# State space layer: the sample states' products in one run over four row groups of the array, and part of the next group's convolution work moved between the squares

## The chip, the cores and the metric

One core of a Trainium2 chip runs the whole program. The metric is device time in microseconds (us), the median of several runs. TensorE multiplies matrices, VectorE and ScalarE do element-wise work, GpSimd does element-wise work and starts some transfers, and SyncE (SP) starts the loads and stores from its queue, in order.

## The reference, cut to what matters

A decoder step of two layers for a prompt (512 tokens) and for 8 samples of 8 new tokens each, which share all weights; all in 32 bit floats. The change is in the state space mixer of the first layer. Per group (8 groups of 4 heads of 64 columns, 128 states):

```python
xc = silu(conv_b + sum(xpad[:, k:k + l] * conv_w[k] for k in range(4)))   # x (two blocks of 128), B, C
xw = (exp(a_cum[:, -1:] - a_cum) * dt)[..., None] * x
states = einsum('bcsgn,bcsgjp->bcgjpn', B, xw)
h = chunk_decay[..., None, None] * h + states        # per sample: the new state, 8 samples of 8 tokens
y = (wts @ x) + (C @ h_prev) * exp(a_cum) + d_skip * x
gz = y * silu(z); gz = gz * rsqrt(mean(gz * gz) + eps) * norm_g
out = gz @ w_out
```

For the samples the state of each of the 8 samples gets the sum over its own 8 tokens of B times the weighted x. The 64 sample tokens lie beside the 512 prompt tokens, 576 columns in all.

## The kernel before, in words

Every engine has its own program; semaphores join them. In the state space stage, `group(g)` is run for 8 groups: 0 by itself, 1 to 6 as a hardware loop ("the middle groups"), 7 by itself. While a group's own work is done, TensorE also projects the next group: six units of weights, `ahead(0)` to `ahead(5)`, 48 products of 288 columns each. It also projects the former group's output back (`back(0)`, `back(1)`, two units). The units' weights come from SP into two raw buffers. ScalarE rounds them (`high_part`, L939, called `proj(k)` for the units of `ahead(k)`). GpSimd takes the rest (`low_part`, L782), and TensorE needs both.

TensorE's order in a middle group is: `decays` (L1764), `back(0)` (L1966 to L1968), `sample_decays` (L1768), `ahead(0)`, `turn` (L1778, L1782), `ahead(1)`, `chunk_sums` (L1790, L1792, L1798), `back(1)`, `ahead(2)`, `outputs` (L1810 to L1833), `ahead(3)`, `states(g, 0)` (L1885), the first half of `ahead(4)`, `group_sums` (L1893), the rest of `ahead(4)`, `states(g, 1)`, `ahead(5)`. In `ahead`, L1523 and L1524 are the products with the rounded weights and L1531 those with the rest.

The 64 sample tokens take rows 0 to 63. A tile `bd` (64 rows, 4 blocks of 128) holds B of each token in one of four blocks and zero in the other three. `states` multiplies it with the weighted x in two row groups of 32 rows (4 samples each). So 8 samples take two calls of four products (each is two records in the trace, since these are 32 bit products), and each call writes banks 6 and 7 of PSUM. VectorE adds them to the states `h0` in between (`sample_states`, L2873). `decays` of the next group waits for the last of these additions, for the root (`gsqrt_ready`) and for `acm`.

At the end of a group: VectorE makes both halves of y (L2855 to L2864), which release ScalarE's squares (L1335); then VectorE takes `ahead(3)` out of PSUM (L2685 to L2687) and adds the squares (L2879, `gsum_done`). TensorE sums over them (L1893), ScalarE takes the root (L1343), VectorE the reciprocal (L2902). Then VectorE scales y, does `sample_states(1)`, `ahead(4)`, the low parts of the result `gl` (L2913), the convolution `conv(g + 1, 2)` and `ahead(5)`. ScalarE's order there: squares, `proj(5)`, root, `conv_out(g + 1, 0)` and `(g + 1, 1)` (L1254, L1258), `tap` 2 and 3 (L1270), `high_part` of the unit for the next `back(0)`, `gh` (L1355), `gate_out`, `conv_out(g + 1, 2)`.

One thread matters across engines. GpSimd's `new_conv_state` (L841) comes behind the low part of `proj(5)`. SP's queue has, in this order: the last unit of the group, the store of that convolution state (L659, waits for L841), the unit for the next `back(0)` (L565), the stores of the states. So that unit can't be asked for before L841 is done.

At the layer's start GpSimd clears the small tiles (L822, L823) once the constants are in, then copies the convolution state, then makes the first low part (L782). VectorE goes through `raw_dt`, the logarithm's series, the sums, `state_coefs`, `token_major` and `head_rows(0)` (L2714, gives `acm`), which the first `decays` waits for.

## Time and profile before

| | |
|---|---|
| time, 3 runs | 2462.85 us median (2460.12 to 2463.0) |
| span of the profiled execution | 2457.2 us |
| median less this span | 5.65 us |
| TensorE busy | 2421.8 us (99% of the span) |
| VectorE, ScalarE, GpSimd busy | 1856.6, 1391.8, 731.7 us |
| mean granted TensorE clock | 0.994 |
| period of a middle group | 66.4 us |

The profile is of one execution. Its span is from the first to the last instruction; of the profiled execution itself no time is given beside its span, so the 5.65 us are what the timed runs have around such a span. PE is TensorE's multiplying, PEld its loading of weights; POOL is GpSimd, DVE VectorE, ACT ScalarE.

### The profile page before, as it was taken

Reading aid. Unit: us, or ns where it says so; the run is one execution under the profiler, and the core shown is the slowest. Engines: PE = TensorE matmul, PEld = TensorE weight load, DVE = VectorE, ACT = ScalarE, POOL = GpSimd, SP = SyncE. Lnnn points to the kernel's source line nnn. Section 1 sums busy time; section 2 is a strip of 40 time slices with the busy share of each in tenths; the row PEclk is TensorE's granted clock in tenths of the full one; section 3 lists DMA queues with packets and bytes.
Section 4 is the critical chain, followed back from the end, with each engine's and each line's share of the span. In section 5 each row is a group of like instructions: output and inputs, shape, how many; then the busy total and the mean of one; then the engine's idle time right before and its main releaser. Section 6 shows DMA issues by size and latency. Waiting matters only on the chain.

```text
span 2457.2 us, 50185 instructions
## 1 busy us (share of the span) xinstructions
PE 2421.8 (99%) x19713; PEld 2363.8 (96%) x19713; DVE 1856.6 (76%) x3053; ACT 1391.8 (57%) x2388; POOL 731.7 (30%) x672
## 2 busy tenths in 40 slices
PE   8999999999999999999999999999999999999998
PEld 8999999889999989999999999999999997999998
DVE  8979767988888888978876988875235438988875
ACT  7757553645555556757665767664222227767663
POOL 1222233444454532222223222224322321222222
PEclk9999999999999998999999999999999999999999
DMA  6677743123333325677665676763443334677762
GB/s 191 163 169 172 167 119 114 47 95 106 105 101 102 97 88 132 167 160 172 159 146 128 161 168 165 173 150 124 157 141 124 136 110 105 161 170 163 173 149 89
DMA packets 105558, 339.00 MB, mean 138 GB/s; under 512 B 13648, under 2 KB 17232, under 8 KB 87056
## 3 DMA queue, kind: packets, MB, share of 16 engines
q1 hardware_dynamic: 53808, 242.38, 30.0%
q0 software_dynamic: 51552, 93.87, 22.7%
q8 instruction: 137, 2.24, 0.4%
q14 instruction: 61, 0.50, 0.1%
HBM read 223.04 MB, written 19.32 MB: 99 GB/s over the span
## 4 chain that ended last, share of the span: by engine, by line
PE 92%; DVE 4%; DMA 1%; ACT 1%; issue 0%; SPq 0%; DVEq 0%; ACTq 0%
PE ps L1627 17%; PE ps L1625 17%; PE ps L1635 17%; PE ps L1523 7%; PE ps L1531 7%; PE ps L1524 7%; PE ps L1644 2%; PE ps L1645 2%; PE ps L1652 2%; PE ps L1966 1%; PE ps L1967 1%; PE ps L1968 1%; PE ps L1574 1%; DMA sb_lw<-sb_rawf 1%; PE ps L1564 1%; PE ps L1565 1%
## 5 line engine op out<-in xcount | busy, mean ns | idle before, releaser
L1627 PE MATMUL ps<-sb_ual,sb_hw 128*128 128x288 f32 x2240 | 612.8, 295 | 0.0
L1625 PE MATMUL ps<-sb_uah,sb_hw 128*128 128x288 f32 x2240 | 609.5, 295 | 0.2
L799 POOL DMA_DIRECT2D sb_lw<-sb_rawf x328 | 282.2, 866 | 961.6 <-ACT sb_lw L970 944.9
L1625 PEld LDWEIGHTS ps<-sb_uah,sb_hw 128*128 128x128 f32 x2240 | 420.9, 188 | 0.9 <-issue 0.7
L1627 PEld LDWEIGHTS ps<-sb_ual,sb_hw 128*128 128x128 f32 x2240 | 421.2, 188 | 0.0
L1635 PE MATMUL ps<-sb_uah,sb_lw 128*128 128x288 f32 x2240 | 384.8, 293 | 1.1 <-DMA sb_lw<-sb_rawf 1.0
L782 POOL TENSOR_TENSOR sb_wl<-sb_raw,sb_wh 128x1024 fp32r<-128x1024 f32 (+1 forms) x106 | 259.2, 2449 | 412.6 <-ACT sb_wh L939 399.0
L1523 PE MATMUL ps<-sb_uh,sb_wh 128*128 128x288 f32 x1360 | 374.2, 302 | 0.4 <-DVE sb_zs L2707 0.2
L1524 PE MATMUL ps<-sb_ul,sb_wh 128*128 128x288 f32 x1360 | 366.6, 296 | 0.0
L1635 PEld LDWEIGHTS ps<-sb_uah,sb_lw 128*128 128x128 f32 x2240 | 327.9, 188 | 2.3 <-DMA sb_lw<-sb_rawf 1.8
L1523 PEld LDWEIGHTS ps<-sb_uh,sb_wh 128*128 128x128 f32 x1360 | 255.7, 188 | 10.3 <-issue 7.0
L968 ACT CAST sb_hw<-sb_rawf 128x512 fp32r<-128x512 f32 x336 | 207.7, 618 | 86.8 <-PE ps L1635 74.9
L1524 PEld LDWEIGHTS ps<-sb_ul,sb_wh 128*128 128x128 f32 x1360 | 255.8, 188 | 0.5
L1627 PE MATMUL ps<-sb_hl,sb_hw 128*128 128x288 f32 x896 | 244.0, 295 | 0.0
L1625 PE MATMUL ps<-sb_hh,sb_hw 128*128 128x288 f32 x896 | 243.2, 294 | 0.0
L939 ACT CAST sb_wh<-sb_raw 128x1024 fp32r<-128x1024 f32 (+1 forms) x106 | 111.9, 1056 | 176.5 <-PE ps L1531 120.8
L2328 DVE TENSOR_TENSOR sb_lw<-sb_tw,sb_hw 128x1024 fp32r<-128x1024 f32 x112 | 137.1, 1224 | 93.3 <-ACT sb_hw L1005 89.1
L970 ACT ACTIVATE sb_lw<-sb_rawf 128x512 fp32r<-128x512 f32 x328 | 206.4, 629 | 0.0
L1531 PE MATMUL ps<-sb_uh,sb_wl 128*128 128x288 f32 x1360 | 195.4, 296 | 0.0
L1005 ACT CAST sb_hw<-sb_tw 128x1024 fp32r<-128x1024 f32 x112 | 117.8, 1052 | 124.1 <-PE ps L1635 124.1
L1531 PEld LDWEIGHTS ps<-sb_uh,sb_wl 128*128 128x128 f32 x1360 | 186.1, 189 | 0.7 <-issue 0.7
L1627 PEld LDWEIGHTS ps<-sb_hl,sb_hw 128*128 128x128 f32 x896 | 168.4, 188 | 0.0
(357 smaller groups left out, 5118.2 us busy)
## 6 DMA issues: line engine op xcount, KB each, us to landing
sb_lw<-sb_rawf POOLq DMA_DIRECT2D x358, 256.0 KB, 3.7
sb_rawf<-w_ffn_in SPq DMA_DIRECT2D x87, 1024.0 KB, 5.0
sb_rawf<-w_ffn_so SPq DMA_DIRECT2D x32, 1024.0 KB, 5.0
sb_raw<-w_ssd SPq DMA_DIRECT2D x64, 512.0 KB, 3.6
sb_raw<-w_att SPq DMA_DIRECT2D x40, 512.0 KB, 3.7
sb_rawf<-w_ffn_out SPq DMA_DIRECT2D x32, 384.0 KB, 3.1
sb_h<-state SPq DMA_DIRECT2D x8, 1024.0 KB, 4.9
ssm_sample<-sb_h SPq DMA_DIRECT2D x8, 1024.0 KB, 4.8
```

The costliest lines, as they stand in the source:

```text
L782: pool.tensor_tensor(wl[parity][:, 0:width], raw[:, parity, 0:width], wh[parity][:, 0:width].bitcast(F32), ALU.subtract).then_inc(wl_done, 1)
L799: pool.dma_start(slot(lw, p), rawf[:, s % 2, i * BL:(i + 1) * BL], accum_op=ALU.add).then_inc(ld_in[i], 16)
L968: nc.scalar.copy(slot(hw, p), src).then_inc(hd_done, 1)
L970: nc.scalar.activation(slot(lw, p), src, ACT.Copy, scale=-1.0).then_inc(nd_done, 1)
L1005: nc.scalar.copy(slot(hw, 7, 2), tw[:, 2 * BL:4 * BL]).then_inc(ht34_done, 1)
L1523: pe.matmul(ps[:, b, 0:n], w, rh[:, k, t0:t0 + n], start=first and k == 0, stop=False)
L1524: pe.matmul(ps[:, b, 0:n], w, rl[:, k, t0:t0 + n], start=False, stop=False)
L1531: ins = pe.matmul(ps[:, b, 0:n], w, rh[:, k, t0:t0 + n], start=False, stop=last and k == nk - 1)
L1625: pe.matmul(out, w[:, k * P:(k + 1) * P], high[k], start=begins and k == 0, stop=False, skip_group_check=True)
L1627: pe.matmul(out, w[:, k * P:(k + 1) * P], low[k], start=False, stop=False, skip_group_check=True)
L1635: ins = pe.matmul(out, v[:, k * P:(k + 1) * P], high[k], start=False, stop=k == 3, skip_group_check=True)
L2328: V.tensor_tensor(slot(lw, 7, 2), tw[:, 2 * BL:4 * BL], slot(hw, 7, 2).bitcast(F32), ALU.subtract).then_inc(lt34_done, 1)
```

## The change

The sample tokens are spread over 128 rows: each sample takes 16 rows, of which 8 hold tokens and 8 are zero. Tiles `xsp` (x) and `bsp` (B) hold them in that form, and ScalarE writes them there in `conv_out`. A row group of 32 rows now holds two samples, `bd` needs two blocks instead of four, and one run of 8 products over four row groups gives all 8 samples' sums, into banks 4 to 7. The run stands behind `ahead(4)`, and waits for the root too, since banks 4 and 5 hold its sums. The other products and VectorE's instructions on sample tokens take 128 rows instead of 64.

In middle groups ScalarE does `conv_out(g + 1, 0)` between the two squares, `conv_out(g + 1, 1)` and `tap` 2 behind them, then the root, and `proj(5)` only behind the root. VectorE adds the squares before it takes `ahead(3)` out, then does `conv(g + 1, 2)`, and then the reciprocal; all four additions to the states come together behind the scaling.

At the layer's start GpSimd clears `xsp` (256 columns), part of `bt` (32 rows, 384 columns) and `bsp` (128 columns). VectorE makes three small copies in `state_coefs` into `bt`, and no longer clears `tok`.

```diff
+            bd = at("bd", [P, 2, NST])
+            xsp = at("xsp", [P, 2, P])
+        def spaced(ap):
+            return ap.rearrange("p (b s) -> p b s", s=2 * NS)[:, :, 0:NS]
+        def samples_of(i):
+            return bsp[:, :] if i == 2 else xsp[:, i, :]
-        def state_bank(half, rg, last):
-            return ((2, 3), (6, 7))[half][rg] if last else 6 + rg
+        def state_bank(rg, last):
+            return (2, 3, 6, 7)[rg] if last else 4 + rg
...
 GpSimd, ssd():
                 pool.memset(cz[:, :], 0.0)
+                pool.memset(xsp[:, :, :].rearrange("p i r -> p (i r)"), 0.0)
+                pool.memset(bt[0:HEADS, 0:3 * P], 0.0)
+                pool.memset(bsp[:, :], 0.0).then_inc(rows_zero, 1)
...
 ScalarE, conv_out and group:
-                    nc.scalar.activation(smp(xc[:, k, SEQ:TOK]), new, ACT.Silu, bias=bias).then_inc(xc_ready, 1)
+                    dst = smp(xc[:, k, SEQ:TOK]) if k == 3 else spaced(samples_of(k))
+                    nc.scalar.activation(dst, new, ACT.Silu, bias=bias).then_inc(xc_ready, 1)
+                    inside = not first and not last
                     for i in range(2):
                         act.wait_ge(gz_ready, g * 2 + (i + 1))
                         nc.scalar.activation(zs[:, i, :], ysb[:, i, :], ACT.Square).then_inc(gsq_done, 1)
-                    if not last:
+                        if inside:
+                            conv_out(g + 1, i)
+                    if inside:
+                        tap(g + 1, 2)
+                    elif first:
                         proj(5)
...
-                    if not last:
+                    if first:
                         conv_out(g + 1, 0)
                         conv_out(g + 1, 1)
                         tap(g + 1, 2)
+                    elif inside:
+                        proj(5)
+                    if not last:
                         tap(g + 1, 3)
...
 TensorE:
-                            ins = pe.transpose(ps[0:SMP, 4, rows(i)], xc[:, i, SEQ:TOK], ident[:, :])
+                            ins = pe.transpose(ps[:, 4, rows(i)], samples_of(i), ident[:, :])
-                    pe.matmul(ps[0:SMP, 4, 0:SMP], xc[:, 2, SEQ:TOK], xc[:, 3, SEQ:TOK],
+                    pe.matmul(ps[:, 4, 0:SMP], samples_of(2), xc[:, 3, SEQ:TOK],
-                def states(g, half, last=False):
+                def states(g, last=False, row_groups=(0, 1, 2, 3)):
...
-                    elif half == 0:
+                    else:
                         pe.wait_ge(y_evac, g * 2 + 2)
-                    else:
-                        pe.wait_ge(ss_evac, g * 4 + 2)
+                        pe.wait_ge(gsqrt_ready, g + 1)
                     for k in range(2):
-                        for rg in range(2):
+                        for rg in row_groups:
...
                     ahead(3)
-                    states(g, 0)
                     ahead(4, lambda: group_sums(g))
-                    states(g, 1)
+                    states(g)
                     ahead(5)
...
 VectorE:
-                    V.memset(tok[:, :, :, :].rearrange("p q c h -> p (q c h)"), 0.0)
-                    V.tensor_tensor(t2, t2, t0, ALU.mult).then_inc(dtok_in, 1)
+                    step(V.tensor_tensor(t2, t2, t0, ALU.mult))
+                    dve.wait_ge(rows_zero, 1)
+                    for q, src in enumerate((acT, t0, t2)):
+                        ins = V.tensor_copy(spaced(bt[0:HEADS, rows(q)]), smp(src[0:HEADS, SEQ:TOK]))
+                    ins.then_inc(dtok_in, 1)
...
-                    if not last:
+                    if first:
                         ahead(3)
...
                         V.tensor_tensor(zs[:, 0, :], zs[:, 0, :], zs[:, 1, :], ALU.add).then_inc(gsum_done, 1)
-                        sample_states(0)
                         if first:
                             conv(1, 1)
                             head_rows(1)
+                        else:
+                            ahead(3)
+                            conv(g + 1, 2)
...
-                        sample_states(1)
+                        sample_states(range(4))
                         ahead(4)
...
-                        conv(g + 1, 2)
+                        if first:
+                            conv(1, 2)
                         ahead(5)
```

## Rows read from the trace of the kernel before

**Rows 1.** The page's part 1: busy time of each engine and share of the span

```profile
PE 2421.8 (99%) x19713; PEld 2363.8 (96%) x19713; DVE 1856.6 (76%) x3053; ACT 1391.8 (57%) x2388; POOL 731.7 (30%) x672
```

**Rows 2.** Waits of TensorE, whole span: us in total, times, longest us

```profile
PE ps L1764 <- DVE sb_acm L2714: 3.6, 1, 3.6
...
PE ps L1764 <- DVE sb_h L2873: 1.1, 1, 1.1
```

**Rows 3.** Window table around groups 0 and 1; PEclk is the granted clock

```profile
434.00:488.00 54.00, 50.21 (x402) 45.97 (x400) 50.36 (x99) 32.92 (x61) 26.79 (x26) 0.97 0.15 43
```

**Rows 4.** The states' products, L1885: all records (ns min/median/max)

```profile
L1885 PEld LDWEIGHTS ps<-sb_xws,sb_bd x128: 181/184/185, 478.5 to 931.6; 32*128 32x128 f32 x128
```

**Rows 5.** TensorE in order of time around a run of `states` (group 1): start, us

```profile
549.59 0.56 PE L1531 MATMUL ps<-sb_uh,sb_wl 128*128 128x288 f32 x3
550.09 1.13 PE L1885 MATMUL ps<-sb_xws,sb_bd 32*128 32x256 f32 x8
...
551.38 0.29 PE L1524 MATMUL ps<-sb_ul,sb_wh 128*128 128x288 f32 x1
```

**Rows 6.** The chain that ended last, pieces in order of time: start, us

```profile
589.03 0.89 PE ps L1790 x8
589.92 0.26 PE ps L1792 x2
```

**Rows 7.** TensorE's weight loads in order of time, group 1 and its end

```profile
553.26 0.82 PEld L1893 LDWEIGHTS ps<-sb_zs,sb_ones 128*128 128x128 f32 x4
...
567.49 0.19 PEld L1966 LDWEIGHTS ps<-sb_gh,sb_wh 128*128 128x128 f32 x1 [0.36 <-issue]
...
574.02 0.18 PEld L1768 LDWEIGHTS ps<-sb_acm,sb_onr 64*128 64x128 f32 x1 [0.17 <-issue]
```

**Rows 8.** VectorE in order of time, end of group 1

```profile
551.00 1.53 DVE L2879 TENSOR_TENSOR sb_zs<-sb_zs 128x576 f32<-128x576 f32 x1
...
555.36 3.75 DVE L2902 RECIPROCAL sb_gnr<-sb_gnr 128x576 f32<-128x576 f32 x1 [1.63 <-ACT sb_gnr L1343]
...
560.70 1.28 DVE L2873 TENSOR_TENSOR sb_h<-sb_h,ps 128x512 f32<-128x512 f32 x2
```

**Rows 9.** ScalarE in order of time, end of group 1 and start of group 2

```profile
549.70 0.69 ACT L1335 ACTIVATE sb_zs<-sb_ysb 128x576 f32<-128x576 f32 x1 [2.15 <-DVE sb_ysb L2864]
...
554.58 0.74 ACT L1343 ACTIVATE sb_gnr<-ps,sb_eps 128x576 f32<-128x576 f32 x1 [1.96 <-PE ps L1893]
...
557.51 0.71 ACT L1254 ACTIVATE sb_xc<-sb_acc,sb_cw 128x512 f32<-128x512 f32 x1
...
560.33 1.05 ACT L939 CAST sb_wh<-sb_raw 128x1024 fp32r<-128x1024 f32 x1 [0.51 <-DMA sb_raw<-w_ssd]
...
572.33 1.14 ACT L1284 ACTIVATE sb_sg<-ps,sb_gtok 128x128 f32<-128x128 f32 x4
```

**Rows 10.** GpSimd in order of time, end of group 1

```profile
554.71 0.66 POOL L841 COPY sb_ncv<-sb_xp 128x27 f32<-128x27 f32 x4
561.47 2.42 POOL L782 TENSOR_TENSOR sb_wl<-sb_raw,sb_wh 128x1024 fp32r<-128x1024 f32 x1 [6.10 <-ACT sb_wh L939]
```

**Rows 11.** SP's queue in order of time, end of group 1

```profile
555.53 0.35 SPq L659 DMA_DIRECT2D conv_new<-sb_ncv  x1
556.47 0.34 SPq L565 DMA_DIRECT2D sb_raw<-w_ssd  x1
```

**Rows 12.** GpSimd, TensorE and VectorE at the layer's start

```profile
396.94 0.31 POOL L823 MEMSET sb_cz<- 128x256 f32 x1
...
397.79 4.76 POOL L782 TENSOR_TENSOR sb_wl<-sb_raw,sb_wh 128x1024 fp32r<-128x1024 f32 x2
...
400.33 0.31 PE L1531 MATMUL ps<-sb_uh,sb_wl 128*128 128x288 f32 x1
...
402.72 0.46 DVE L2685 TENSOR_TENSOR sb_xp<-ps,sb_rms 128x288 f32<-128x288 f32 x1 [1.92 <-PE ps L1531]
...
441.17 0.24 DVE L2676 COPY sb_tok<-ps 64x96 f32<-64x96 f32 x1
```

More of the change, by code:

```diff
@@ L266, in step_kernel @@
             mask = at("mask", [P, P])
-            masks = at("masks", [SMP, SMP])
-            maskb = at("maskb", [SMP, NB // 2])
+            masks = at("masks", [P, SMP])
+            maskb = at("maskb", [P, 2])
+            at("pad_mb", [P, 2])
             cz = at("cz", [P, NB * 32])
-            at("pad_h0", [P, 320])
+            bsp = at("bsp", [P, P])
+            at("pad_h0", [P, 320 - P])
             h0 = at("h0", [P, NB, HPG * PD])
@@ L1369, in ssd @@
                 high_part(0, 8, U_GRP + 6, UW)
+                act.wait_ge(rows_zero, 1)
                 gate_out(0, 0)
@@ L1870, in last_outputs @@
                         ins.then_inc(y_mm, 1)
-                def states(g, half, last=False):
+                def states(g, last=False, row_groups=(0, 1, 2, 3)):
                     if last:
-                        pe.wait_ge(so_evac, g * 8 + 1)
-                        if half:
-                            pe.wait_ge(y_evac, g * 2 + 2)
-                    elif half == 0:
+                        pe.wait_ge(*((y_evac, g * 2 + 2) if 2 in row_groups else (so_evac, g * 8 + 1)))
+                    else:
                         pe.wait_ge(y_evac, g * 2 + 2)
-                    else:
-                        pe.wait_ge(ss_evac, g * 4 + 2)
+                        pe.wait_ge(gsqrt_ready, g + 1)
                     for k in range(2):
-                        for rg in range(2):
+                        for rg in row_groups:
                             r = slice(32 * rg, 32 * rg + 32)
-                            ins = pe.matmul(ps[:, state_bank(half, rg, last), k * 256:k * 256 + 256], bd[r, 2 * half + k, :],
+                            ins = pe.matmul(ps[:, state_bank(rg, last), k * 256:k * 256 + 256], bd[r, k, :],
                                             xws[r, :, :].rearrange("p j d -> p (j d)"), start=True, stop=True)
@@ L1978, in ssd @@
                     for c in range(CH + 1):
-                        n = P if c < CH else SMP
+                        tokens = src[:, rows(c)] if c < CH else bt[0:HEADS, rows(q)]
                         col = (q * (CH + 1) + c) * HEADS
-                        ins = pe.transpose(ps[0:n, 4, col:col + HEADS], src[:, c * P:c * P + n], ident[0:HEADS, 0:HEADS])
+                        ins = pe.transpose(ps[:, 4, col:col + HEADS], tokens, ident[0:HEADS, 0:HEADS])
                 ins.then_inc(dtok_mm, 1)
@@ L2034, in ssd @@
                 last_outputs(g)
-                states(g, 0, True)
+                states(g, True, (0, 1))
                 token_sums(g, 0)
-                states(g, 1, True)
+                states(g, True, (2, 3))
                 token_sums(g, 1)
@@ L2674, in token_major @@
                     v = ps[:, 4, 0:3 * (CH + 1) * HEADS].rearrange("p (q c h) -> p q c h", q=3, c=CH + 1)
-                    V.tensor_copy(tok[:, :, 0:CH, :], v[:, :, 0:CH, :])
-                    V.tensor_copy(tok[0:SMP, :, CH, :], v[0:SMP, :, CH, :])
+                    V.tensor_copy(tok[:, :, :, :], v)
                     step(V.tensor_copy(acT[:, :], acm[:, 0, :].bitcast(F32)))
@@ L2776, in group @@
                     for q, dst in ((1, xds), (2, xws)):
[L2777 to L2781 removed]
+                        V.tensor_tensor(dst[:, :, :], ps[:, 4, 0:2 * P].rearrange("p (j d) -> p j d", j=HPG),
+                                        gtok[:, q, CH, :].unsqueeze(2).broadcast_to([P, HPG, PD]), ALU.mult)
+                    both = [P, 2, NST]
+                    V.tensor_tensor(bd[:, :, :], ps[:, 4, 2 * P:3 * P].unsqueeze(1).broadcast_to(both),
+                                    maskb[:, :].unsqueeze(2).broadcast_to(both), ALU.mult).then_inc(xs_done, 1)
                     def states():
@@ L2864, in group, with sample_states @@
                         V.tensor_tensor(ysb[:, i, :], ysb[:, i, :], zs[:, i, :], ALU.mult).then_inc(gz_ready, 1)
-                    if not last:
+                    if first:
                         ahead(3)
-                    def sample_states(half, row_groups=(0, 1)):
-                        dve.wait_ge(ss_mm, g * 2 + half + 1)
+                    def sample_states(row_groups):
+                        dve.wait_ge(ss_mm, g + (2 if 2 in row_groups and last else 1))
                         for rg in row_groups:
-                            b = 4 * rg + 2 * half
+                            b = 2 * rg
                             dve.wait_ge(hm_done, g * 8 + b + 2)
-                            V.tensor_tensor(h0[:, b:b + 2, :], h0[:, b:b + 2, :], two(ps[:, state_bank(half, rg, last), :]),
+                            V.tensor_tensor(h0[:, b:b + 2, :], h0[:, b:b + 2, :], two(ps[:, state_bank(rg, last), :]),
                                             ALU.add).then_inc(ss_evac, 1)
@@ L3192, in constants @@
         "ones": np.ones((P, P), f), "ident": np.eye(P, dtype=f), "mask": np.triu(np.ones((P, P), f)),
-        "mask_smp": (np.triu(np.ones((SMP, SMP))) * (s[:, None] // NS == s[None, :] // NS)).astype(f),
-        "mask_block": (s[:, None] // NS % (NB // 2) == np.arange(NB // 2)[None, :]).astype(f),
+        "mask_smp": ((a[:, None] // 16 == s[None, :] // NS) * (a[:, None] % 16 <= s[None, :] % NS)).astype(f),
+        "mask_block": (a[:, None] // 16 % 2 == np.arange(2)[None, :]).astype(f),
         "keep": np.tile(keep, (H2, 1)), "one_head": np.tile(np.eye(HEADS, dtype=f), (2, 1)), "dist": np.concatenate(tables, 1).astype(f),
```

34 lines of the change are left out of this document (14 added, 20 removed).

## The prediction

> **What bounds the kernel now.** The busy table first: TensorE is busy for 99% of the span [rows 1]. So a microsecond comes only from three places: TensorE's own work, its waits, and its clock. Its waits are the second view [rows 2]. They are few, and none of the long ones is in the middle groups: 3.6 us for `acm` before the first `decays`, and 1.1 us for the additions to the states before group 1. In a middle group TensorE never waits, so what the change takes from it there counts in full, and any delay elsewhere is free up to its slack. The third view, engine by engine in order of time at the end of a group, gives the slacks; I do it in group 1, in the clock of the trace.
>
> **The states' products.** Now: two runs of 8 records in each group. Three L1531 records take 0.56 us of which the last one's length is 0.29, so they follow each other by 0.135, and the last begins at 549.86; L1524 behind the run begins at 551.38; without the run it would be two records of 0.135 later, so a run costs 551.38 - 549.86 - 0.27 = 1.25 us [rows 5]. Can one run do the work of two? One weight load takes 0.184 us [rows 4]; eight in a row would be 1.47 us, and the whole run is 1.13 us [rows 5]: the two row groups already load and multiply at the same time, in four waves. Sixteen records over four row groups are again four waves. So I take 1.25 us for the merged run and 1.25 us as saved. The bound on the other side is that four row groups go no faster than two: then the merged run takes some 1.1 us more and only 0.15 us is saved. The row is nearer to the first, since the loads of different row groups overlap.
>
> The Trainium skill ("TensorE: Matmul & The Clock Gate", the part on packing small matmuls) reports 3.07 times the speed, not 4, for four row groups; by an estimate from that figure the merged run would be longer by a tenth of a microsecond or two. No run here shows it yet, and the sum doesn't use it.
>
> **Smaller changes of shape.** L1792 now has 64 columns of weights between shapes of 128: 0.26 us for two records, where two of L1790's are 0.22 [rows 6]; the change of shape beside it goes too. Bounds: 0 and 0.26 saved; I take 0.2. The transposes and the samples' y products I take at nothing: as many records as before, between neighbours of the same kind. On VectorE and ScalarE 128 rows cost what 64 do; I take nothing, and `bd` gets shorter.
>
> **What comes too late in a middle group.**
> - The sum of squares. TensorE reaches L1893's load at 553.26 - 1.25 = 552.01 [rows 7]. The second square ends at 549.70 + 0.69 = 550.39 [rows 9], the addition takes 1.53 us [rows 8]: 551.97, and a little for the semaphore. No slack is left; I take 0.1 us of wait, bounds 0 and 0.3. `conv_out(g + 1, 0)` lies in ScalarE's 2.15 us of idle time before the second square [rows 9], so it costs nothing.
> - The root now begins 554.58 - 553.26 = 1.32 us behind that load [rows 9, 7], at 553.4. ScalarE is free by then: it gets a `conv_out` (0.71 and a small one) and a tap of about as many columns, loses a cast of 1.05, and had 1.96 us to spare [rows 9].
> - The cast for `ahead(5)` stands behind the root now: 553.4 + 0.7 + 1.05 = 555.15. GpSimd's low part takes 2.42 us, its four copies 0.66 [rows 10]: 558.25. Now they end at 554.71 + 0.66 = 555.37. `ahead(5)` itself is not late (TensorE comes to it some six microseconds behind L1893's load, with the rounded part first). What is late is what SP has queued behind: store at 558.4 and the unit for the next `back(0)` at 559.35 instead of 556.47 [rows 11]. ScalarE already waits for that unit now, 0.51 us, and casts it at 560.33 [rows 9]. With 2.9 us more: cast from 563.2 to 564.25, low part from 564.3 to 566.75. `back(0)` needs the low part before its first product; TensorE's load for it is at 567.49 now [rows 7], and 1.25 - 0.1 earlier then: 566.35. So TensorE waits 0.4 us, every time. I take 0.45; bounds: 0 (the load lands sooner) and 1.5 (it lands among the stores).
> - VectorE isn't late: conv(2) fills the 1.63 us it waits for the root now, so the reciprocal begins at 555.4 as before; four additions instead of two end 1.3 us later than 561.98 [rows 8], at 563.3. `decays` is four records ahead of L1966's load, about a microsecond ahead of 566.35. Slack some 1.8 us.
> - The store of the states goes with that last addition, 1.3 us later, and the next weights are queued behind it. In the next group `sample_decays` needs the first L1284 at 573.47 [rows 9] and comes at 574.02 [rows 7]. TensorE is some 0.7 us earlier there and ScalarE is not. I take 0.15 of wait, bounds 0 and 0.7.
>
> Net of a middle group: 1.25 + 0.2 - 0.1 - 0.45 - 0.15 = 0.75 us. Six groups: 4.5 us.
>
> **Group 0.** Its last wait is for VectorE's additions before `decays` of group 1, 1.1 us [rows 2]. The change leaves VectorE the same work up to there, in another order, so what TensorE saves by the merged run becomes a longer wait: 0, apart from L1792's 0.2. Group 7 keeps its two runs of states: 0, bound 0.3 faster for the shorter `bd`.
>
> **The start of the layer.** The clearing of 256 columns took from 396.94 to 397.20, 0.26 us [rows 12]. The new ones (256, 384 and 128 columns) are then about 0.26 + 0.37 + 0.13 = 0.76 us, ahead of the first low part. This ends at 397.79 + 4.76 / 2 = 400.17, and TensorE takes it at 400.33 [rows 12]: nothing hides the clearing, TensorE loses about 0.7 us. VectorE waits 1.92 us for that very product [rows 12] and then has the chain that ends in `acm`, for which TensorE waits 3.6 us [rows 2]; so these 0.7 us reach the end of that wait. The three copies lie in the same chain: about 0.15 us each by the copy of 96 columns (0.24 with its tail [rows 12]), 0.45; one copy fewer behind gives back under 0.1, and the clearing of `tok` was under ScalarE's exponential, so it gives nothing. Together 1.15 us lost; bounds 0.4 and 1.4.
>
> **The sum.** 4.5 + 0.2 - 1.15 = 3.55 us, with 0.3 us for the unpriced small gains 3.85. The profiled execution has a span of 2457.2 us, and the median is 5.65 us more; I take the same 5.65 us around the new span, 2453.35: 2459.0 us.
>
> **The rivals.**
> - *The unit for back(0) is not late.* For it: loads of this kind vary, and the lead of 0.45 us is small against 2.9 us of shift. Then also less slips behind: 6 x 0.6 = 3.6 us more, 2455.4 us.
> - *Four row groups don't run together.* Against it: the overlapping loads [rows 4, 5]; for it: no row has four. The 1.1 us lost per group also makes TensorE late enough that no wait arises: 1.25 + 0.2 - 1.1 = 0.35, six times 2.1, less 0.95: gain 1.15, 2461.7 us.
> - *The chain through GpSimd and SP is a microsecond longer than I have it.* The wait at `back(0)` grows to 1.45: 6 us more, 2465 us. From 1.95 us of wait on it would be a loss that shows.
> - *The additions to the states become the bound.* The Trainium skill ("TensorEngine Tiling (Array Packing)", PSUM bottleneck) warns that the emptying of PSUM then limits. Here the slack worked out above is 1.8 us; past it every microsecond counts six times. With 0.8 us past it: 2463.8 us.
> - *The clock, on the other side.* Around groups 0 and 1, with waits of 3.6 and 1.1 us, the granted clock is 0.97 over 54 us [rows 3], a loss of 1.6 us. If three short waits in each middle group brought that down each time: 6 x 1.6 = 9.6 us, 2468.6 us, slower. Against it: only waits of over a microsecond stand ahead of that stretch. It decides from five groups on.
>
> **How the numbers follow.** A measurement of this kernel can tell about 0.2%, 4.9 us, from no change: under 2457.9 is faster, over 2467.8 slower. Chances: my forecast 0.45, spread over 2456.5 to 2461.5; back(0) not late 0.2; row groups not together 0.1; longer chain 0.1; additions 0.05; clock 0.06; anything else on the slow side 0.04. Faster: 0.2, and 0.2 of the forecast's own spread: 0.4. Slower: the clock, half of the longer chain's tail and the rest, 0.1. Same: 0.5. The range of eight in ten reaches from the second case with its spread to the longer chain: 2454.0 to 2465.0.
>
> **What the profile would show.** One run of 16 records at L1885 per group, no longer than 1.3 us; L1893 loading at once behind a half of `ahead(4)`, or waiting for `sb_zs`; the first load of L1966 waiting for `sb_wl` for some 0.4 us in each group; L841 ending 2.9 us later; the first low part at the layer's start waited for by TensorE, 0.7 us, and the wait for `acm` at 4.0. The forecast is wrong if the merged run takes over 2 us, if L1966 never waits, or if the granted clock falls in the middle groups.

## The result and the profile after

The changed kernel takes 2473.03 us (median of 4 runs, 2471.87 to 2476.65), the kernel before 2461.48 beside it: a ratio of 1.0047 with a 95% interval of 1.0032 to 1.0061. It is slower by some 12 us, clear of noise, where I had forecast 2459.0 (2454.0 to 2465.0) and gave a slower kernel a chance of 0.1. The profiled execution has a span of 2470.0 us, 12.8 over the one before.

The page's first part, after, answers to [rows 1]:

```profile
PE 2423.5 (98%) x19713; PEld 2370.5 (96%) x19713; DVE 1858.8 (75%) x3054; ACT 1393.2 (56%) x2388; POOL 733.4 (30%) x675
```

TensorE's busy time is about what it was, though 1.25 us of products per group are gone; so it worked slower somewhere, and it waited more. The waits of TensorE over the whole span, after (us in total, times, longest), answer to [rows 2]:

```profile
PE ps L1987 <- DVE sb_gl L2937: 8.3, 6, 1.5
...
PE ps L1788 <- DVE sb_acm L2736: 3.5, 1, 3.5
PE ps L1788 <- DVE sb_h L2895: 3.3, 1, 3.3
...
PE ps L1914 <- DVE sb_zs L2901: 1.9, 7, 0.3
```

The first line is new: six times, at `back(0)`, TensorE waits for `gl`. The third was 1.1 us. A line of the kernel before, hidden by the dots of [rows 2], has gone:

```profile
PE ps L1966 <- DVE sb_zs L2707: 2.0, 1, 2.0
```

That was a wait inside group 1 (at 501.0), for VectorE to empty a bank that the next product of `back(0)` needs. So "In a middle group TensorE never waits" held for groups 2 to 6 only. The window table over the middle groups (TensorE's busy time and records, granted clock, DMA share, GB/s), of the kernel before and then of the one after:

```profile
500.00:900.00 400.00, 398.95 (x3146) 1.00 0.31 99
```

```profile
500.00:900.00 400.00, 391.24 (x3108) 0.98 0.29 94
```

TensorE gets through fewer records in the same 400 us, and the granted clock is 0.98 there instead of 1.00. The clock's own records say where: half clock for 3.4 us each from 568.0, 704.5, 772.8, 841.1 and 909.3 us, each time beside a wait at `back(0)` (groups 2, 4, 5, 6 and 7); and for 6.8 us from 496.3, at the start of group 1, where the kernel before has 3.4 us from 502.4. TensorE in order of time around the first of them answers to [rows 5] and [rows 7]:

```profile
557.85 1.15 PE L1906 MATMUL ps<-sb_xws,sb_bd 32*128 32x256 f32 x16
...
565.52 1.20 PE L1788 MATMUL ps<-sb_acm,sb_onr 64*128 64x512 f32 x4
568.18 0.61 PE L1987 MATMUL ps<-sb_gh,sb_wh 128*128 128x288 f32 x1 [1.47 <-DVE sb_gl L2937]
...
569.55 0.44 PE L1989 MATMUL ps<-sb_gh,sb_wl 128*128 128x288 f32 x1
569.79 0.44 PE L1987 MATMUL ps<-sb_gh,sb_wh 128*128 128x288 f32 x1
...
571.72 0.29 PE L1987 MATMUL ps<-sb_gh,sb_wh 128*128 128x288 f32 x1
571.85 0.29 PE L1988 MATMUL ps<-sb_gl,sb_wh 128*128 128x288 f32 x1
```

The merged run of 16 records takes 1.15 us, as forecast. Then 1.47 us of wait, and behind it the records follow each other by 0.24 us (1.2 GHz), and from 571.5 on by 0.13 (2.4 GHz). One lap of the group, from its first `decays` to the next group's, takes 68.39, 66.87, 68.41, 68.43 and 68.43 us for groups 2 to 6; before, 66.42, 66.49, 66.41, 66.50 and 66.41. The lap of 66.87 is the one without a stretch at half clock.

Now the other engines at the end of group 1. VectorE, answering to [rows 8]:

```profile
550.22 2.13 DVE L2901 TENSOR_TENSOR sb_zs<-sb_zs 128x576 f32<-128x576 f32 x1 [0.75 <-ACT sb_zs L1351]
...
554.05 1.83 DVE L2720 SCALAR_TENSOR_TENSOR sb_acc<-sb_xp,sb_cw,sb_acc 128x600 f32<-128x600 f32 x2 [0.15 <-DVE sb_acc L2720]
555.80 3.74 DVE L2926 RECIPROCAL sb_gnr<-sb_gnr 128x576 f32<-128x576 f32 x1
...
561.13 2.47 DVE L2895 TENSOR_TENSOR sb_h<-sb_h,ps 128x512 f32<-128x512 f32 x4
...
565.74 3.06 DVE L2937 TENSOR_TENSOR sb_gl<-sb_ysb,sb_gh 128x576 fp32r<-128x576 f32 x2 [1.47 <-ACT sb_gh L1378]
```

ScalarE, answering to [rows 9]:

```profile
553.68 0.74 ACT L1363 ACTIVATE sb_gnr<-ps,sb_eps 128x576 f32<-128x576 f32 x1 [0.65 <-PE ps L1914]
554.32 1.04 ACT L953 CAST sb_wh<-sb_raw 128x1024 fp32r<-128x1024 f32 x1
...
564.02 1.05 ACT L953 CAST sb_wh<-sb_raw 128x1024 fp32r<-128x1024 f32 x1 [7.96 <-DMA sb_raw<-w_ssd]
564.97 1.24 ACT L1378 CAST sb_gh<-sb_ysb 128x576 fp32r<-128x576 f32 x2
566.23 1.28 ACT L1277 ACT_TABLE_LOAD   x1
```

GpSimd, answering to [rows 10]:

```profile
548.81 2.92 POOL L793 TENSOR_TENSOR sb_wl<-sb_raw,sb_wh 128x1024 fp32r<-128x1024 f32 x1
555.44 2.70 POOL L793 TENSOR_TENSOR sb_wl<-sb_raw,sb_wh 128x1024 fp32r<-128x1024 f32 x1 [3.71 <-ACT sb_wh L953]
558.09 0.66 POOL L855 COPY sb_ncv<-sb_xp 128x27 f32<-128x27 f32 x4
565.14 2.37 POOL L793 TENSOR_TENSOR sb_wl<-sb_raw,sb_wh 128x1024 fp32r<-128x1024 f32 x1 [6.40 <-ACT sb_wh L953]
```

SP's queue, answering to [rows 11]:

```profile
558.91 0.35 SPq L670 DMA_DIRECT2D conv_new<-sb_ncv  x1
559.85 0.33 SPq L576 DMA_DIRECT2D sb_raw<-w_ssd  x1
560.36 0.36 SPq L646 DMA_DIRECT2D ssm_prompt<-sb_hst  x1
563.77 0.36 SPq L650 DMA_DIRECT2D ssm_sample<-sb_h  x1
564.40 3.63 SPq L576 DMA_DIRECT2D sb_raw<-w_ssd  x2
```

Read from the last fence upward: the unit of `back(0)` is asked for at 559.85, behind the `conv_new` store, behind the copies (L855), behind the low part of `ahead(5)`, behind its cast at 554.32, behind the root. ScalarE is idle for 7.96 us until it lands, casts it, and casts `gh` behind it. Then VectorE's first `gl` starts at 565.74 and ends at 568.13, 2.39 us for an operation that takes 0.75 by itself: it ends 0.6 us behind GpSimd's low part (567.51). TensorE begins at 568.18. It was free at 566.71, so 0.8 of its 1.47 us of wait passed until the low part's end, and 0.67 from there to the end of `gl`.

The start of the layer, on GpSimd and on VectorE, answers to [rows 12]:

```profile
396.33 0.31 POOL L834 MEMSET sb_cz<- 128x256 f32 x1
396.58 0.31 POOL L835 MEMSET sb_xsp<- 128x256 f32 x1
396.83 0.41 POOL L836 MEMSET sb_bt<- 32x384 f32 x1
397.19 0.19 POOL L837 MEMSET sb_bsp<- 128x128 f32 x1
```

```profile
402.86 0.46 DVE L2707 TENSOR_TENSOR sb_xp<-ps,sb_rms 128x288 f32<-128x288 f32 x1 [2.35 <-PE ps L1555]
...
431.88 0.18 DVE L2687 COPY sb_bt<-sb_acT 32x64 f32<-32x64 f32 x1
```

Where the 12.8 us of the two profiled executions lie, by the first `decays` of each group: 0.45 up to the first (444.37 against 443.92), 1.2 in group 0 (53.20 against 52.04), -2.45 in group 1 (67.95 against 70.40), 8.3 in groups 2 to 6, 2.3 from group 7's `decays` to the first product of `spread` (40.0 against 37.7), and 3.1 behind it, in layers that the change doesn't touch. The last piece is between 1517.7 and 1524.0 us in the profiles that I compared (before, after, e4, e6, e10, e11, e13, e14, e15), in no order that goes with the kernel's time: scatter of single executions.

The first piece, too, is mixed with scatter of the part ahead of the layer: GpSimd comes to the clearing of `cz`, right ahead of the new clears, at 396.33 instead of 396.94. From that clearing to the first `decays` it is 48.04 us against 46.98, so the start of the layer loses 1.06 us. The other runs agree: 46.97 to 47.04 in the three kernels with the old layout (before, e5, e10), 48.02 to 48.06 in all ten that have the three clears there.

### The profile page after: what moved, and what is told of

Read it like the earlier page. It is cut to its first block, busy times and chain, and to the rows that moved or that the text cites. A ratio compares the mean times of both kernels' runs of the same rounds, so it can differ in the third digit from the quotient of the medians.

```text
span 2470.0 us, 50196 instructions
## 1 busy us (share of the span) xinstructions
PE 2423.5 (98%) x19713; PEld 2370.5 (96%) x19713; DVE 1858.8 (75%) x3054; ACT 1393.2 (56%) x2388; POOL 733.4 (30%) x675
## 4 chain that ended last, share of the span: by engine, by line
PE 83%; DVE 8%; issue 3%; DMA 2%; ACT 2%; POOL 1%; SPq 0%; DVEq 0%; ACTq 0%; POOLq 0%
PE ps L1651 16%; PE ps L1649 16%; PE ps L1659 16%; PE ps L1547 5%; PE ps L1555 5%; PE ps L1548 4%; PE ps L1668 2%; PE ps L1669 2%; PE ps L1676 2%; PE ps L1987 2%; PE ps L1989 1%; PE ps L1988 1%; PE ps L1598 1%; DVE sb_acc L2720 1%; DMA sb_raw<-w_ssd 1%
## 5 line engine op out<-in xcount | busy, mean ns | idle before, releaser
L1649 PEld LDWEIGHTS ps<-sb_hh,sb_hw 128*128 128x128 f32 x896 | 168.1, 188 | 0.5 <-issue 0.5
```

The lines of the kernel that those rows point to most:

```text
L1649: pe.matmul(out, w[:, k * P:(k + 1) * P], high[k], start=begins and k == 0, stop=False, skip_group_check=True)
```

## The experiments

All were timed beside the kernel before (2460.4 to 2460.7 us). Three theories at first: A, the late unit of `back(0)`; B, VectorE and GpSimd in each other's way; C, the new layout itself.

**e1: the cast of `ahead(5)` back behind the second square**, so that nothing of the chain to the unit stands behind the root.

```
 nc.scalar.activation(zs[:, i, :], ysb[:, i, :], ACT.Square)...
+if i and not last:
+    proj(5)
 if inside:
     conv_out(g + 1, i)
...
-elif inside:
-    proj(5)
```

> The changed kernel, but in the middle groups ScalarE casts the unit of ahead(5) right behind the second square, ahead of conv_out(g + 1, 1), tap 2 and the root, instead of behind the root. Theory A (late unit: the cast behind the root delays GpSimd's low part, L841, SP's store and the unit for back(0) queued behind it): that unit is asked for some 3 us earlier, the wait of about 1.4 us ahead of back(0) is gone in all six groups, the clock stays at 1.00 there, and the time is 2455 to 2459 us. Theory B (what counts is that VectorE's gl and GpSimd's low part fall together): the same, since the low part is over sooner. Theory C (the spaced layout itself costs): the wait may go, but the time stays above 2466 us.

Measured: 2474.11 us, 1.0061 [1.0048, 1.0073]. No half-clock stretch is left in groups 2 to 6, the wait at `back(0)` falls to 0.4 us, and yet a lap takes 68.05 us, and the time is 15 us over what theory A gave. TensorE's waits in e1, whole span:

```profile
PE ps L1790 <- ACT sb_sg L1299: 11.5, 6, 2.0
...
PE ps L1985 <- DVE sb_gl L2935: 2.3, 6, 0.5
```

A new wait of 1.9 us, at `sample_decays` (L1790 there), for ScalarE. Its cause, in VectorE's, SP's and ScalarE's rows of e1:

```profile
553.15 3.76 DVE L2718 SCALAR_TENSOR_TENSOR sb_acc<-sb_xp,sb_cw,sb_acc 128x600 f32<-128x600 f32 x2 [0.15 <-DVE sb_acc L2718]
556.83 3.74 DVE L2924 RECIPROCAL sb_gnr<-sb_gnr 128x576 f32<-128x576 f32 x1
...
562.16 2.47 DVE L2893 TENSOR_TENSOR sb_h<-sb_h,ps 128x512 f32<-128x512 f32 x4
```

```profile
564.80 0.36 SPq L650 DMA_DIRECT2D ssm_sample<-sb_h  x1
565.43 1.58 SPq L576 DMA_DIRECT2D sb_raw<-w_ssd  x2
```

```profile
570.92 1.05 ACT L953 CAST sb_wh<-sb_raw 128x1024 fp32r<-128x1024 f32 x1 [2.61 <-DMA sb_raw<-w_ssd]
```

There is a second unit in SP's queue, that of `ahead(0)`, behind the store of the samples' states, and that store waits for VectorE's last addition. The additions stand behind the reciprocal, and this now stands behind `conv(g + 1, 2)`: it starts 3.0 us after the root's end here (556.83 against 553.84), and 1.4 in the change and in e2, instead of at once. The unit is cast at 570.92, ahead of the exponentials in ScalarE's order, and these are what `sample_decays` waits for.

**e2: SP asks for the unit of `back(0)` ahead of the `conv_new` store.**

```
 part(0, io["w_ssd"][g - 1, 6])
+store_conv(g)
 store_prompt(g - 1)
...
-store_conv(g + 1)
```

> The changed kernel, but SP's queue asks for the unit of the next back(0) ahead of the store of the convolution state, which moves behind it. ScalarE's order stays as changed. Theory A: the unit no longer waits for L841 and lands before 560, the wait ahead of back(0) is gone, the clock stays, 2455 to 2459 us. If the cast behind the root hurts in another way than through SP's queue (ahead(5) itself late, or the store late), the time stays above 2465 us. Theory C: above 2466 us.

Measured: 2473.81 us, 1.0051 [1.0038, 1.0064]. Again 15 us over. The unit is asked for at 549.97 and `back(0)` waits no more in groups 2 to 7; the laps of groups 2 to 6 are 69.0 to 70.6 us, with a half-clock stretch in each. TensorE's waits in e2:

```profile
PE ps L1792 <- ACT sb_sg L1299: 13.5, 6, 2.3
```

The same second wait as in e1, by another way to it. Theory A alone falls.

**e4: the new layout with the orders of before on ScalarE and VectorE. e5: the new orders on the layout of before.** e4 takes the hunks of ScalarE's and VectorE's order out of the change, e5 puts them alone into the kernel before:

```
-inside = not first and not last
+inside = False
...
-if first:
+if not last:
     ahead(3)
...
-else:
-    ahead(3)
-    conv(g + 1, 2)
...
-if first:
-    conv(1, 2)
+conv(g + 1, 2)
 ahead(5)
```

> The spaced rows and the one run over four row groups alone; ScalarE and VectorE go in the order of the kernel before in the middle groups (without the first additions to the states). Theory A: no late unit; TensorE waits up to 0.6 us for the sum of squares, since VectorE takes ahead(3) out ahead of it; some 0.7 us gained per group, less the longer start of the layer: 2456 to 2460 us. Theory C: 2465 us or more.

> The new order of ScalarE and VectorE in the middle groups alone, on the old layout (64 rows, two runs of states; the first two additions to the states stay behind the sum of squares). Theory A: the unit for back(0) is late here too, but TensorE comes 1.3 us later, so the wait is 0.2 to 0.8 us in six groups, no gain beside it: 2462 to 2467 us. Theory C: as the kernel before or a little faster, 2459 to 2462 us.

Measured: e4 2457.72 us, 0.9987 [0.9979, 0.9996], laps 65.7 to 65.9; e5 2476.71 us, 1.0069 [1.0057, 1.0081], laps 68.7 to 69.8. Theory C falls: the layout is a gain, and all of the loss is the orders'. But e5 is 10 us over my upper bound. I had TensorE come 1.3 us later to `back(0)` on the old layout and wait that much less; it waits 1.5 to 1.7 us six times. The run that the new layout saves stands ahead of the products for the sum of squares, and the late chain starts behind these: from them to where TensorE is free for `back(0)` it is 14.15 us in e5 (553.00 to 567.15) and 14.31 in the change (552.40 to 566.71). An earlier TensorE takes the chain with it.

From here I had theory D: two late units in a row, of which each hides the other. Its rivals were E (the order on ScalarE costs by itself: Silu's table is loaded again behind `gh`, 1.28 us at 566.23), L (VectorE held by GpSimd, what was B) and F (the clock).

**e6: SP asks for both units ahead of all three stores**, in the middle groups.

```
 part(0, io["w_ssd"][g - 1, 6])
+part(1, io["w_ssd"][g + 1, 0])
+store_conv(g)
 store_prompt(g - 1)
 store_samples(g - 1)
-part(1, io["w_ssd"][g + 1, 0])
...
-store_conv(g + 1)
```

> The change, with SP's order in the middle groups altered: the units for back(0) and ahead(0) are asked for ahead of the three stores (conv_new, ssm_prompt, ssm_sample). Theory D (two late units in a row: back(0)'s behind the conv_new store, and ahead(0)'s behind the ssm_sample store, which waits for VectorE's last addition; when the first was mended, in e1 and e2, the cast of the second, and the exponentials behind it on ScalarE, became late, and TensorE waited 2 us at sample_decays instead): no wait over 0.3 us at back(0) or at sample_decays, group period 65.7 to 66.2 as in e4, time 2457 to 2460. Theory E (the order on ScalarE costs by itself: the table of Silu is loaded again behind the casts of gh, 1.28 us in the tight stretch): the exponentials still start 1.3 us later than in e4, waits of about 1 us at sample_decays, period 67 or more, time 2464 to 2468.

Measured: 2456.94 us, 0.9988 [0.9978, 0.9997]. Neither wait is left in the middle groups; laps 65.33 or 65.34, which makes 13.9 us in groups 2 to 6 alone. The window over them:

```profile
500.00:900.00 400.00, 397.33 (x3189) 0.99 0.31 99
```

With the orders on ScalarE and VectorE untouched, 16 us come back by one block of SP's queue. Theory D held; the table load is still there and costs nothing, so E falls for the middle groups.

**e7: `conv(g + 1, 2)` alone back behind `gl`. e8: that, and SP's order of e2.**

```
 ahead(3)
-conv(g + 1, 2)
...
 V.tensor_tensor(gl[:, i, :], ...)
+conv(g + 1, 2)
 ahead(5)
```

> The change, with VectorE's conv(g + 1, 2) alone back in its old place (behind the subtractions gl). Theory D: the reciprocal starts right behind the root (1.3 us earlier), so the last addition ends 3.2 us ahead of the decays instead of 1.9, and the unit of ahead(0) is asked for earlier; but the cast of ahead(5) and its low part stay behind the root, so the unit of back(0) is still late and TensorE still waits 1.0 to 1.5 us at back(0): period 67.3 to 68.4, time 2467 to 2473. If conv(2) ahead of the reciprocal were the whole cause: period 65.8, time 2458.

> The change, with conv(g + 1, 2) back behind gl and, on SP, the conv_new store behind the unit of back(0) (as in e2). Theory D: each edit mends one of the two late units, and together they give what neither e2 nor the edit before gives alone: no wait over 0.5 us at back(0) or sample_decays, period 65.7 to 66.5, time 2457 to 2461. If the two were independent small losses, or the ScalarE order itself costs (theory E): period 67 or more, time 2464 or more.

Measured: e7 2481.77 us, 1.0088 [1.0072, 1.0104], 9 us over my upper bound; e8 2463.27 us, 1.0010 [1.0002, 1.0019], 2 us over. Laps 69.0 to 70.7 and 67.0 to 67.1 us. I had left out what stands behind `conv(g + 1, 2)` then. TensorE's waits in e7, 500 to 900 us:

```profile
PE ps L1987 <- DVE sb_zs L2729: 11.0, 5, 2.2
PE ps L1987 <- DVE sb_gl L2936: 5.5, 5, 1.2
```

The late `gl` now pushes conv(2), 2.7 us, and the evacuation of `ahead(5)` (L2729) behind it, and the next product of `back(0)` needs that bank: a second wait of 2.2 us. In e8 it is 8.4 us in six (1.45 in each of groups 2 to 6), the larger part of the 1.7 us by which a lap of 67.1 is over e6's. So the early `conv(g + 1, 2)` both costs (the additions) and pays (the bank), and taking it back is no cure.

**e9: GpSimd's low parts of `ahead(0)`, `ahead(4)`, `ahead(5)` and `back(0)` over half of their columns** in the middle groups; the other half of that part of the computation is left out.

```
-low_part(..., u % 2, UW)
+low_part(..., u % 2, UW // 2)
```

> The change, but in the middle groups GpSimd forms the low part of only half of the columns of the units of ahead(0), ahead(4), ahead(5) and back(0) (that part of the computation is left out; the products still run over the whole width). Theory L (a VectorE operation that reads two tiles in SBUF can't start until the GpSimd tensor_tensor that is running has ended): the addition of the squares falls from 2.13 to 0.8 us, the first gl from 2.39 to about 1.2 us, back(0) waits 0 to 0.5 us instead of 1.5, low part 1.2 to 1.5 us; period 65.9 to 67, time 2457 to 2465. Without L (both were long for another reason): the addition stays at 2.1 and gl at 2.4 us, and only the earlier low part of ahead(5) gives 1.3 us at the unit of back(0): back(0) still waits 1 us or more.

Measured: 2455.58 us, 0.9977 [0.9968, 0.9987], 1.4 us under my range, laps 64.9 to 65.0. GpSimd and VectorE at the end of a group of e9:

```profile
615.88 1.81 POOL L793 TENSOR_TENSOR sb_wl<-sb_raw,sb_wh 128x512 fp32r<-128x512 f32 x1
```

```profile
617.28 1.02 DVE L2901 TENSOR_TENSOR sb_zs<-sb_zs 128x576 f32<-128x576 f32 x1 [0.75 <-ACT sb_zs L1351]
```

The addition of the squares takes 1.02 us instead of 2.13, and ends 0.6 us behind the end of the low part again (618.30 against 617.69). Theory L holds for the durations. That e9 is the quicker by 17 us is both things at once, a low part that is over sooner and VectorE set free; it doesn't part them.

**e10: the kernel before with SP's order of e6. e11: e4 with that order.** The diff is that of e6, on these two kernels.

> The kernel before, with SP's order alone altered as in e6 (units for back(0) and ahead(0) asked for ahead of the three stores). Theory D: in the kernel before both units arrive in time, so the order is worth nothing there: 2459 to 2462, same as before. If SP's order were a gain of its own, of which e6's time is made, it would be 2457 or less here.

> e4 (new layout, the orders of before on ScalarE and VectorE) with SP's order of e6. Theory D: e4 has no late unit, so 2456.5 to 2458.5, group period 65.7; set beside e6 it says what the new orders are worth once nothing waits for SP: e6's groups took 65.34 us, so 65.7 here gives 0.4 us a group to the orders. If SP's order is what shortened them, 65.3 here too.

Measured: e10 2456.58 us, 0.9989 [0.9980, 0.9998]; e11 2453.42 us, 0.9976 [0.9965, 0.9987]; both 2 to 3 us under my ranges. Here theory D was too narrow: SP's order is worth 4 us by the medians in the kernel before as well (2.7 by the ratio). Not in the middle groups (laps 66.4 to 66.5 as before), but around groups 0 and 1: the wait of 1.1 us for the additions ahead of group 1's `decays` is gone, the one inside group 1 is 1.7 us instead of 2.0, and no half-clock stretch stands where it stood at 502.4 us; group 1's lap is 68.52 instead of 70.40. The rows show how the first wait goes. VectorE's scaling of y, which reads tiles in SBUF (the engines' working memory), takes 3.34 us for its two steps in the kernel before, beside GpSimd's low part of the unit for `back(0)` (490.87 to 493.27), and 1.77 us in e10, where that unit comes earlier and its low part is over at 491.36. The additions stand behind it. In e11 the middle laps are 65.34 or 65.35, the same as in e6.

**e12: the change with six products that nobody reads** in front of the wait at `back(0)` in the middle groups.

```
+if m == 0 and not isinstance(g, int):
+    keep_busy(6)
 if m % 4 == 0:
     pe.wait_ge(wl_done, u + 1)
```

> The change, with six products of 128 columns whose result nobody reads, issued by TensorE ahead of its wait at back(0) in the middle groups: they fill about 1.3 us of the 1.5 us for which it waits. Theory F (the stretches of 3.4 us at half clock that follow this wait, at 568, 705, 773, 841 and 909 us, come from the idle time of TensorE): they are gone, the groups take 66.9 us as the one group of after without such a stretch, time 2463 to 2467. Rival: the clock falls for another reason (the periods of 68.4 stay): 2472 to 2475. Where the products run past the wait they cost some tenths a group.

Measured: 2465.39 us, 1.0026 [1.0016, 1.0035]; laps 66.7, 66.9, 66.8, 66.6 and 66.9, no half-clock stretch in groups 2 to 6. The window over them:

```profile
500.00:900.00 400.00, 396.80 (x3190) 0.99 0.29 96
```

`gl` comes as late as in the change, only the idle time is filled, and the five laps are together 333.9 us instead of 340.5: 6.6 us come back, four stretches of some 1.55 us and a little. (By the medians against the kernel before it is 6.7, by the ratios 5.2.) The stretches left are in group 1, which makes the 0.99, and in group 7, whose wait isn't filled. Theory F holds: with group 7's, some 8 of the 12 us that the change loses (five stretches of 1.55, an estimate) are the clock's answer to the waits and not the waits.

**e13: e6 with the three clears behind GpSimd's second low part of the layer. e14: e13 with SP's order in the last group too. e15: e14 with the orders of before on ScalarE and VectorE (e4's edit).** After e11 it was open why e6 stays 3.5 us behind it though their middle groups are equal. Its waits of TensorE showed where:

```profile
PE ps L1792 <- ACT sb_sg L1299: 2.0, 1, 2.0
```

Once, in the last group, whose part of SP's queue e6 had left alone. The edits of e13 and, below the dots, e14:

```
 low_part(U_GRP + k, (U_GRP + k) % 2, UW)
+if k == 1:
+    pool.memset(xsp[:, :, :].rearrange("p i r -> p (i r)"), 0.0)
+    pool.memset(bt[0:HEADS, 0:3 * P], 0.0)
+    pool.memset(bsp[:, :], 0.0).then_inc(rows_zero, 1)
...
 unit(U_TAIL, U_TAIL % 2, io["w_ssd"][g - 1, 6], UW)
+unit(U_TAIL + 1, (U_TAIL + 1) % 2, io["w_ssd"][g - 1, 7], UW)
+store_conv(g)
 store_prompt(g - 1)
 store_samples(g - 1)
-unit(U_TAIL + 1, (U_TAIL + 1) % 2, io["w_ssd"][g - 1, 7], UW)
```

> e6 with GpSimd's three clears of the spaced rows moved behind the second low part of the layer's first group, where GpSimd has time. The first decays, 0.45 us later in after than in before, come 0.4 us earlier: 2456.5, ratio 0.0002 under e6's, which these rounds can hardly tell; if the clears only pushed something else back, as e6 or above.

> The changed orders once more: e13 (the two units ahead of the stores in the middle groups, clears later) with the same order on SP in the last group, where e6 still waits 2.0 us at sample_decays and takes 40.7 us from its decays to the last spread, against 36.9 in e11. Theory D: the wait goes and this stretch falls to 37.5 to 38.5: 2452 to 2453.5. Then nothing is left of the loss of after, and beside the next kernel it shows what the new orders are worth by themselves. Theory E (the new orders cost 3 us whatever SP does): as e13 or above, 2454.5 to 2456.

> The new layout with the orders of before on ScalarE and VectorE, the clears later and SP's order altered in the middle groups and in the last. Theory D: e11 has no late unit in the last group, so that edit gives nothing, the clears 0.4: 2453, within 0.05% of e14, since the new orders are worth nothing where TensorE doesn't wait. Theory E: 2 to 3 us under e14.

Measured: e13 2454.64 us, 0.9980 [0.9971, 0.9989]; e14 2451.22 us, 0.9964 [0.9950, 0.9977]; e15 2452.24 us, 0.9964 [0.9951, 0.9978]. The stretch from group 7's `decays` to `spread` falls from 40.7 us in e6 to 37.3 in e14, where e15 has 36.9. e13 gives the 0.4 us of the clears by its rows (47.66 us from the clearing of `cz` to the first `decays`, against 48.06 in e6); its time is more than I expected under e6's, 2.3 us, which the intervals hardly tell from that. e14 and e15 are the same as far as five runs of each can tell (each interval reaches some 3.3 us to either side), and their middle laps are 65.3 to 65.4 us in both: with all units in time the new orders show no worth and no cost. Both beat both kernels.

## Why the prediction was wrong

- *The merged run*: right. Its 16 records take 1.15 us where 8 took 1.13, and by the forecast's own reckoning, from the last record ahead of it to the second behind it, it costs 559.16 - 557.62 - 0.27 = 1.27 us (forecast 1.25); the rival that four row groups don't run together fell. With nothing in the way (e6, e11) a lap is 65.34 us against 66.45, so the layout is worth 1.1 us a group; I had 1.45 before waits, and 0.1 of wait for the squares (measured 0.3, bounds 0 to 0.3).
- *The sum of squares*: the earlier start of the addition (550.22 against 551.00) bought nothing, as it ends at the same distance behind GpSimd's low part: 552.35, before 552.53. I took the duration 1.53 us from the row as a price of the operation; the second `gl`, a VectorE operation of the same size, takes 0.75 us with GpSimd at rest, so half of the 1.53 was waiting. (550.39 + 1.53 is 551.92, not 551.97; nothing hangs on it.)
- *The late unit of `back(0)`*: the chain was right link by link and I had it 0.8 us too short: unit at 559.85 (forecast 559.35), cast at 564.02 (563.2), low part done at 567.51 (566.75). That alone makes the rival "a longer chain".
- **The failed step, first half: "So TensorE waits 0.4 us, every time. I take 0.45".** I let the wait end with the low part. What ends last is `gl`: it is behind the late cast of `gh`, so it meets GpSimd's low part and is held until 0.6 us after its end. The wait was 1.4 to 1.5 us in groups 2 to 6, at the edge of my bound of 1.5: up to the low part's end it would have been 0.8, which is the longer chain, and the other 0.67 is the step that the sum didn't have.
- **The failed step, second half: the clock, at which I gave 0.06.** "Against it: only waits of over a microsecond stand ahead of that stretch" was a reason that depended on the 0.45 us. With waits of 1.5 us the condition for the rival was met: five stretches of some 1.55 us each (68.41 - 66.87). e12 shows it. The row that I took the price from was also misread: its window, 434 to 488, holds the wait of 3.6 us alone. The second stretch at half clock of the kernel before, at 502.4, stood behind waits of 1.1 and 2.0 us, so a stretch behind a wait inside a middle group was there to be seen. The two rivals weren't independent, and I had priced them as if they were: the longer chain brings the clock with it, and by my own figures the two together are 2465 + 9.6 = 2474.6 us. That this is near the 2473.03 measured is half luck: it has six longer waits and six stretches in groups 1 to 6, some 11 us lost there, and the profiles have 5.9, the rest lying in groups 0 and 7 and in the scatter behind.
- *"VectorE isn't late: conv(2) fills the 1.63 us it waits for the root now"*: `ahead(3)` and conv(2) begin only when the held addition has ended, so the reciprocal starts 1.4 us after the root's end in the change, where it started at once, and the four additions end at 563.61, 1.6 us later than before. I had 1.3. My 1.8 us of slack was reckoned against `decays`; the use that counts is SP's, whose next unit is behind the store. I gave this 0.15 us "bounds 0 and 0.7"; uncovered, in e1 and e2, it is 1.9 to 2.3 us. In the change it didn't show only since TensorE was already late by the other wait.
- *Group 0*: forecast 0.2 us gained, measured 1.2 lost; the wait for the additions ahead of group 1's `decays` grew from 1.1 to 3.3 us. "The change leaves VectorE the same work up to there, in another order" is what didn't hold here. In the kernel before, two additions ran while GpSimd was at a low part (480.90 to 482.17); now `conv` stands there and is held (its first step takes 2.95 us, the next 0.84), the reciprocal starts no earlier (487.58 against 487.50), and four additions come behind it. The scaling ahead of them is held as well, beside GpSimd's low part from 491.41 to 494.42:

```profile
491.35 3.69 DVE L2929 SCALAR_TENSOR_TENSOR sb_ysb<-sb_ysb,sb_ng,sb_gnr 128x576 f32<-128x576 f32 x2
```

  In e6, where SP asks for the unit earlier and its low part ends at 494.15, the two steps start at 494.03 and take 1.55 us. These 2.1 us are what e6's wait of 1.2 is shorter by; e4, with SP's order as it was, has 3.63 us of scaling and a wait of 3.2. But the longer wait isn't a loss in full: with it the 2.0 us of wait inside group 1 goes. The two together were 3.07 us and are 3.33, and group 1's lap is 2.45 us shorter.
- *Group 7*: forecast 0, measured 2.3 lost, by the same wait at `back(0)` (1.2 us) and a half-clock stretch at 909.3.
- *The start of the layer*: right. Forecast 1.15 us lost, measured 1.06 from the clearing of `cz` on. VectorE takes its first product 0.75 us later from there (6.53 us behind that clearing, 5.78 before), for 0.76 forecast, and the three copies make the rest, about 0.3 together.
- *The 5.65 us around the span*: the median is 3.0 us over the profiled span after. The profiled execution after took 2471.87 us, 1.9 over its own span, so most of the 5.65 was how far one execution lay under the median. The span was forecast at 2453.35 and measured at 2470.0, 16.7 us off; the median is 14.0 off.
- *A slip in the rivals*: "it decides from five groups on" is wrong by its own figures; five groups of 1.6 us give 2467.0, under the 2467.8 that would show.

The loss is settled as two late units plus the clock: each has a run that takes it away (e6, e14; e12). Open is what decides whether the clock falls behind a wait; why e4's laps are 0.4 us over e11's, of which its rows show 0.2 of wait for a bank that VectorE empties later, behind a held `gl`; and the part of e9's gain that is the hold alone.

## What to carry to other kernels

When a step moves behind another on one engine, follow it to the queue that issues transfers, and look at every transfer behind it there, not only the first: a store that waits for a late result holds back the loads behind it, and a second late load is hidden as long as the first is later. Here the cure was the order of SP's queue, loads ahead of stores. A duration in a row is no price of the operation where another engine may have held it: compare it with the shortest of its shape. And where a new wait of TensorE comes to 1.5 us, price with it what the clock may take behind it, which here was as much again in five of six groups, and nothing in e8.

## What the runs showed of the hardware

A VectorE operation that reads two tiles in SBUF was held while GpSimd's `tensor_tensor` ran. Four sightings, each ending 0.6 us behind GpSimd's end, and the scalings and the `conv` step of group 0 besides: `gl` 2.39 us for 0.75, the addition of squares 2.13 in the change and 1.02 in e9, and a step of `conv` in e1 (L2718, 2.74 us at 621.22 for the 0.83 of the step before it, GpSimd's low part until 623.3). The additions to the states, which read one of their two tiles from PSUM (the banks of TensorE's results), followed each other by 0.6 us beside a running low part too (552.45 and 553.05 in the kernel before, low part 551.88 to 554.77). The Trainium skill ("SBUF — State Buffer", "SBUF: two separate sides") states this as a rule: an operation with two SBUF inputs and one of GpSimd that reads SBUF exclude each other for the whole instruction. The traces agree.

The clock fell to 1.2 GHz for 3.4 us beside waits of only 1.5 us, in five of the six groups that have such a wait in the change. The length of one wait doesn't decide it: in e1 TensorE waits 1.9 to 2.0 us at `sample_decays` in six groups and one stretch stands beside such a wait (915.3), in e2 it waits 2.2 to 2.3 us and five do, in e8 1.45 us at `back(0)` in groups 2 to 7 and none does. What decides it no run here shows.

Four row groups of 32 rows ran 16 records in 1.15 us, two took 1.13 us for 8.
